# The second norm by token halves, the second modulation's folds moved, and two gate panels in other banks

## The reference

```python
sh1, sc1, g1, sh2, sc2, g2 = jnp.split(jax.nn.silu(c) @ w_mod[l] + b_mod[l], N_MOD, axis=-1)
...
y_att = attend(q, k, v) @ lw['w_attn_o']
y_conv = conformer_conv(u, lw)
merged = jax.nn.sigmoid(ga) * y_att + jax.nn.sigmoid(gc) * y_conv
return merged @ lw['w_out']
...
xs = xs + g1 * token_mixer(hx, lw, rope, k_c, v_c)
hx = modulate(rmsnorm(xs, norm2_g[l]), sh2, sc2)
xs = xs + g2 * peer_ffn(hx, lw)
```

## Time and profile before

| | |
|---|---|
| median of 3 runs | 2541.25 us (2539.21 to 2551.24) |
| the profiled execution: its own time | 2543.47 us |
| its span | 2541.7 us |
| TensorE, VectorE, ScalarE, GpSimd busy | 96%, 66%, 36%, 29% |
| mean granted clock of TensorE | 0.986 |

### The profile page before, as it was taken

One profiled execution on the slowest core, in us unless ns is written; L12 is line 12 of the kernel. 1 busy time (PEld: TensorE's weight loads), 2 busy tenths in 40 slices (PEclk: granted clock), 3 DMA queues, 4 the chain that ended last, 5 costly groups with the idle time before them and its releaser, 6 DMA issues.

```text
span 2541.7 us, 34943 instructions
## 1 busy us (share of the span) xinstructions
PE 2445.8 (96%) x12016; PEld 2073.1 (82%) x12016; DVE 1682.9 (66%) x3129; ACT 911.3 (36%) x1308; POOL 743.7 (29%) x646
## 2 busy tenths in 40 slices
PE   6999999998999999999999999999999989999998
PEld 4877887786887878888777899999999766788886
DVE  4887768788666676777632378888887784444434
ACT  4223852523233333333322333333333564222222
POOL 0000000000025666666675347777741000000000
PEclk8999999999999999999999999999999999999999
DMA  6322913353234444444455589999997212222231
GB/s 256 100 75 98 341 50 127 138 191 141 83 129 137 140 143 140 149 137 145 139 163 166 191 272 363 366 361 359 361 365 279 83 34 67 91 95 95 99 98 59
DMA packets 177222, 433.60 MB, mean 171 GB/s; under 512 B 32752, under 2 KB 81904, under 8 KB 176752
## 3 DMA queue, kind: packets, MB, share of 16 engines
q1 hardware_dynamic: 123888, 331.61, 38.2%
q0 software_dynamic: 34816, 67.41, 7.6%
q10 hardware_dynamic: 18432, 33.56, 3.5%
HBM read 371.48 MB, written 61.01 MB: 170 GB/s over the span
## 4 chain that ended last, share of the span: by engine, by line
PE 82%; DVE 9%; another core or an unknown queue 3%; issue 2%; ACT 2%; DMA 1%; ACTq 0%; SPq 0%; DVEq 0%
PE ps L478 16%; PE ps L480 16%; PE ps L479 16%; PE ps L829 8%; PE ps L831 8%; PE ps L830 8%; DVE wlo L1534 2%; PE ps L736 2%; DVE ar L1587 1%; PE ps L708 1%; ACT whi L1014 1%; PE ps L726 1%; PE ps L548 1%; PE ps L550 1%
## 5 line engine op out<-in xcount | busy, mean ns | idle before, releaser
L1534 DVE TENSOR_TENSOR wlo<-raw,whi 128x1024 fp32r<-128x1024 f32 x426 | 521.4, 1224 | 605.6 <-ACT whi L1014 515.2
L2446 POOL DMA_INDIRECT w_scratch<-ar x384 | 420.9, 1096 | 953.4 <-DVE wlo L1534 849.2
L1014 ACT ACTIVATE whi<-raw 128x1024 fp32r<-128x1024 f32 x424 | 448.8, 1059 | 662.5 <-PE ps L831 348.9
L478 PE MATMUL ps<-b_hi,whi 128*128 128x512 f32 x1312 | 515.8, 393 | 15.8 <-DVE wlo L1534 15.6
L480 PE MATMUL ps<-b_hi,wlo 128*128 128x512 f32 x1312 | 512.6, 391 | 0.8 <-issue 0.8
L479 PE MATMUL ps<-b_lo,whi 128*128 128x512 f32 x1312 | 512.4, 391 | 0.0
L829 PE MATMUL ps<-a_hi,whi 128*128 128x384 f32 x1024 | 344.4, 336 | 6.1 <-issue 3.7
L831 PE MATMUL ps<-a_hi,wlo 128*128 128x384 f32 x1024 | 343.2, 335 | 0.0
L830 PE MATMUL ps<-a_lo,whi 128*128 128x384 f32 x1024 | 343.2, 335 | 0.0
L478 PE MATMUL ps<-a_hi,whi 128*128 128x512 f32 x808 | 323.3, 400 | 6.0 <-DVE wlo L1534 3.3
L480 PE MATMUL ps<-a_hi,wlo 128*128 128x512 f32 x808 | 316.0, 391 | 0.0
(11 more groups left out here) (270 smaller groups left out, 2928.9 us busy)
## 6 DMA issues: line engine op xcount, KB each, us to landing
raw<-panels SPq DMA_DIRECT2D x430, 512.0 KB
w_scratch<-rstd SPq DMA_DIRECT2D x32, 768.0 KB, 10.7
ar<-w_scratch SPq DMA_DIRECT2D x128, 192.0 KB
ar<-gelu_scratch SPq DMA_DIRECT2D x128, 192.0 KB
ar<-mod SPq DMA_DIRECT2D x32, 512.0 KB, 5.3
gelu_scratch<-ar ACTq DMA_DIRECT2D x64, 256.0 KB
gelu_scratch<-sq ACTq DMA_DIRECT2D x32, 256.0 KB
gelu_scratch<-nt ACTq DMA_DIRECT2D x32, 256.0 KB
```

The costliest lines, as they stand in the source:

```text
L478: pe.matmul(bank, w_h, hi[:, k, :], start=(k == 0), stop=False)
L1014: act.activation(whi[:, u % SPLIT, :], raw[:, u % RAW, :], ACT.Copy).then_inc(hi_ready, 1)
L1534: dve.tensor_tensor(wlo[:, u % SPLIT, :], raw[:, u % RAW, :], f32(whi[:, u % SPLIT, :]), ALU.subtract).then_inc(lo_ready, 1)
L2446: nc.gpsimd.indirect_dma_start(experts, bass.IndirectOffsetOnAxis(offs[:, k:k + 1], 0), vals[:, k:k + 1], None)\
```

## The change

Three things change, in one stretch of the program.

1. Gate panels 6 and 7 go to banks 5 and 4, those of the layer norm's sums, and so wait for `cv_stat` and `cv_rt` and for no released gate bank beyond that of panel 5.
2. The folds of the second modulation move forward: pair 4 ahead of the `w_conv_o` loop, pairs 5 to 8 in its turns 0 to 3, pair 9 in turn 5, pairs 10 to 13 in turns 0 to 3 of the `w_out` loop. `mod2_sums(0)` to `(5)` move forward with them, and SP's table `pair_at` too.
3. `w_out` panels 6 and 7 are done by halves of 256 tokens, in the order 6 first half, 7 first half, 6 second half, 7 second half, in four banks (2, 3, 5, 6). The norm's sums, roots, reciprocals, tiles and the first two query panels follow by halves. SP's wait for the keys counts both halves (`4 * KT`); the numbers of later norms go up by one.

The diff, cut to what the prediction speaks of:

```diff
@@ -318,6 +319,10 @@
...
 
+        def gc_bank(k):
+            return k if k < 4 else k - 4 if k < 6 else 11 - k
         def mod2_bank(n):
@@ -409,7 +418,7 @@
...
 
-            pair_at = {3: 2, 4: 3, 8: 4, 9: 5, 11: 6, 12: 7, 13: 8, 14: 9, 19: 10, 20: 11, 21: 12, 22: 13, 23: 14, 24: 15}
+            pair_at = {3: 2, 4: 3, 8: 4, 9: 5, 10: 6, 11: 7, 12: 8, 13: 9, 14: 10, 16: 11, 19: 12, 20: 13, 22: 14, 24: 15}
             for n in range(2 * KT + 4):
@@ -420,7 +429,7 @@
...
 
-            sp.wait_ge(h_ready, 3 * KT)
+            sp.wait_ge(h_ready, 4 * KT)
             sp.dma_start(keys, keys_d).then_inc(keys_in, 16)
@@ -483,27 +492,36 @@
...
 
+            def half_total(half):
+                cols = slice(half * HT, (half + 1) * HT)
+                pe.wait_ge(sq_used, 2 * KT + 6)
+                pe.matmul(ps[:, 4, cols], ones, rstd[:, cols], start=True, stop=False)
+                pe.wait_ge(sq_ready, (3 + half) * KT)
+                pe.matmul(ps[:, 4, cols], ones, sq[:, 0, cols], start=False, stop=False)
+                pe.matmul(ps[:, 4, cols], ones, sq[:, 1, cols], start=False, stop=True).then_inc(sq_used, 8 if half else 2)
             def two_panels(g, hi, lo, free, ready):
 
-                def tile(u, k):
-                    if k == 0:
+                def tile(u, k, half):
+                    cols = slice(half * HT, (half + 1) * HT)
+                    if k == 0 and half == 0:
                         pe.wait_ge(lo_ready, g + u + (1 - U))
...
                     if u == 0:
-                        pe.wait_ge(ready[0], ready[1] + k + 1)
-                    w_h = whi[:, u, k * P:(k + 1) * P]
-                    w_l = wlo[:, u, k * P:(k + 1) * P]
-                    pe.matmul(ps[:, u, :], w_h, hi[:, k, :], start=(k == 0), stop=False)
-                    pe.matmul(ps[:, u, :], w_h, lo[:, k, :], start=False, stop=False)
-                    last = pe.matmul(ps[:, u, :], w_l, hi[:, k, :], start=False, stop=(k == KT - 1))
-                    if k == KT - 1:
+                        pe.wait_ge(ready[0], ready[1] + half * KT + k + 1)
+                    last = split3(ps[:, u, cols], u, k, hi[:, k, cols], lo[:, k, cols], k == 0, k == KT - 1)
+                    if k == KT - 1 and half:
                         last.then_inc(used, 1)
 
-                for s in range(KT + LAG):
-                    if s < KT:
-                        tile(0, s)
-                    if s >= LAG:
-                        tile(1, s - LAG)
+                for half in range(2):
+                    for s in range(KT + LAG):
+                        if s < KT:
+                            tile(0, s, half)
+                        if s >= LAG:
+                            tile(1, s - LAG, half)
+                        if half == 0 and s == 4:
+                            half_total(1)
 
@@ -772,25 +795,39 @@
...
             for k in range(2, KT):
+                if k == 6:
+                    pe.wait_ge(cv_stat, 1)
+                    pe.wait_ge(cv_rt, 1)
                 gate_panel(k)
-            def mod2_sums(q):
-                pe.wait_ge(folds2, (q + 1) * 2 * KT)
-                for n in range(4 * q, 4 * q + 4):
-                    pe.matmul(ps[:, mod2_bank(n), n:n + 1], fold2[:, n % 8, :], ones[:, 0:1], start=True, stop=True).then_inc(summed2, 1)
-            mod2_sums(0)
+                if k == 5:
+                    mod2_sums(0)
+            mod2_sums(1)
             for k in range(KT):
                 panel(CO + k, k % 4, ps[:, k % 4, :], b_hi, b_lo, r_of(CO) + k + 1, (cv_ready, 0) if k == 0 else None)
-                if k in (1, 3, 5):
-                    mod2_sums((k + 1) // 2)
-            for k in range(KT):
+                if k in (2, 4):
+                    mod2_sums(1 + k // 2)
+            def wo_half(k, half):
+                cols = slice(half * HT, (half + 1) * HT)
+                if half == 0:
+                    pe.wait_ge(lo_ready, WO + k + (1 - U))
+                    pe.wait_ge(bank_free, r_of(WO) + k + 1)
+                elif k == KT - 1:
+                    pe.wait_ge(mod_done, 5)
+                for d in range(KT):
+                    last = split3(ps[:, wo_bank(k, half), cols], k, d, a_hi[:, d, cols], a_lo[:, d, cols], d == 0, d == KT - 1)
+                    if d == 3 and k == KT - 2 and half:
+                        half_total(0)
+                last.then_inc(used if half else wo_half_done, 1)
+            for k in range(KT - 2):
                 panel(WO + k, k, ps[:, k % 4, :], a_hi, a_lo, r_of(WO) + k + 1, (m_ready, 0) if k == 0 else None)
-                if k in (3, 5):
-                    mod2_sums((k + 5) // 2)
-            norm_total(2, rstd[:, :])
+                if k in (0, 3):
+                    mod2_sums(4 + k // 3)
+            for half in range(2):
+                for k in (KT - 2, KT - 1):
+                    wo_half(k, half)
             pe.wait_ge(mod_done, 4)
@@ -1286,18 +1323,48 @@
...
 
-            for k in range(KT):
+            for k in range(KT - 1):
                 hi_next(k // 4, WO, k % 4)
...
                     act.activation(tiny[:, 50:51], col("zero"), ACT.Sqrt)
-            act.wait_ge(x_ready, KT)
-            sum_sq_tile(2, KT - 1, rstd[:, :])
-            norm_root(2, rstd[:, :])
+            def half_sq(k, half):
+                cols = slice(half * HT, (half + 1) * HT)
+                act.wait_ge(x_ready, (KT if half else KT - 2) + k - (KT - 2) + 1)
+                act.wait_ge(sq_used, 2 * KT + k - 1)
+                act.activation(sq[:, k % 2, cols], x[:, k, cols], ACT.Square).then_inc(sq_ready, (6 if k == KT - 2 else 2) if half else 1)
+            def half_root(half):
+                cols = slice(half * HT, (half + 1) * HT)
+                act.wait_ge(sq_used, (3 + half) * KT)
+                act.activation(rstd[:, cols], ps[:, 4, cols], ACT.Sqrt, bias=EPS, scale=1.0 / D).then_inc(rt_ready, 1)
+            def half_hi(k, half):
+                cols = slice(half * HT, (half + 1) * HT)
+                act.wait_ge(nt_ready, (2 + half) * KT + k + 1)
+                act.activation(b_hi[:, k, cols], nt[:, k % 2, cols], ACT.Identity, bias=mod[:, 3 * KT + k, 0:1]).then_inc(nhi_ready, 1)
+            half_sq(KT - 2, 0)
+            half_sq(KT - 1, 0)
+            half_root(0)
+            hi_next(1, WO, 3)
+            half_hi(0, 0)
+            half_hi(1, 0)
+            half_sq(KT - 2, 1)
+            half_hi(2, 0)
+            half_hi(3, 0)
+            half_hi(4, 0)
+            half_sq(KT - 1, 1)
             hi(WQ + 1, 1, ((WQ + 1) // 4 + ROUNDS) * 16)
-            norm_hi(2, b_hi, lambda k: mod[:, 3 * KT + k, 0:1])
+            half_hi(5, 0)
+            half_hi(6, 0)
+            half_root(1)
+            half_hi(7, 0)
+            for k in range(KT):
+                half_hi(k, 1)
 
@@ -1888,7 +1955,7 @@
...
             lo(CO + 1, 1)
+            fold_half(2, 0)
 
@@ -1906,7 +1973,9 @@
...
                 if k < 4:
-                    fold_half(2 + k // 2, k % 2)
+                    fold_half((5 + k) // 2, (5 + k) % 2)
+                if k == 5:
+                    fold_half(4, 1)
             merged_lo(KT - 1)
@@ -1932,24 +2001,79 @@
...
 
-            for k in range(KT):
-                if k < KT - 1:
-                    lo(WO + k + 2, k + 2)
+            for k in range(KT - 2):
+                lo(WO + k + 2, k + 2)
                 if k > 1:
...
                 dve.sem_inc(bank_free, 1)
-                if k < 6:
-                    fold_half(4 + k // 2, k % 2)
-                if k == 6:
-                    add_mod2(KT, 2 * KT)
-                    dve.wait_ge(mod_done, 5)
-                    dve.scalar_tensor_tensor(gs2[:, :], mod[:, 4 * KT:5 * KT, 0], 1.0, col("norm2", 0, KT), ALU.add, ALU.mult).then_inc(mod_done, 1)
-                    dve.wait_ge(mod_done, 6)
-            norm_rstd(2)
-            norm_apply(2, x, lambda k: gs2[:, k:k + 1], lambda k: mod[:, 3 * KT + k, 0:1], b_hi, b_lo, middle=lambda: lo(WQ + 1, 1))
+                if k < 4:
+                    fold_half((10 + k) // 2, k % 2)
+            add_mod2(KT, 2 * KT)
+            dve.wait_ge(mod_done, 5)
+            dve.scalar_tensor_tensor(gs2[:, :], mod[:, 4 * KT:5 * KT, 0], 1.0, col("norm2", 0, KT), ALU.add, ALU.mult).then_inc(mod_done, 1)
+            dve.wait_ge(mod_done, 6)
+            add_sq(2, 5, rstd[:, :])
+            def half_add(k, half):
+                cols = slice(half * HT, (half + 1) * HT)
+                if half:
+                    dve.wait_ge(used, WO + k + 1)
+                else:
+                    dve.wait_ge(wo_half_done, k - (KT - 2) + 1)
+                dve.scalar_tensor_tensor(x[:, k, cols], ps[:, wo_bank(k, half), cols], mod[:, 2 * KT + k, 0:1], x[:, k, cols], ALU.mult, ALU.add).then_inc(x_ready, 1)
+                if half:
+                    dve.wait_ge(x_ready, KT + k - (KT - 2) + 1)
+                    dve.sem_inc(bank_free, 1)
+            def half_norm(k, half):
```

(42 more changed lines are left out.)

67 lines of the change are left out of this document (37 added, 30 removed).

## The result

| | before | after |
|---|---|---|
| median of 20 runs each, side by side | 2551.3 us (2539.21 to 2555.88) | 2557.66 us (2542.72 to 2566.78) |
| the profiled execution: its own time, its span | 2543.47, 2541.7 us | 2563.92, 2562.1 us |
| mean granted clock of TensorE | 0.986 | 0.983 |

The ratio is 1.0037, with a 95% interval of 1.0025 to 1.0049: slower, by less than the 0.5% that I had named as telling. Two things are to be kept apart. The median of before, 2541.25 of three runs when the prediction was made, is 2551.3 over twenty, so 10 of the 17 us between forecast and median say nothing of the change. But the sign is wrong as well: forecast -0.6, measured +6.4 as the difference of the two medians, and +9.4 by the ratio.

What follows compares the result with a forecast made beforehand. TensorE, busy for 96% of the span, was taken as the bound, so only pauses and clock could be saved. Delays carried through the stretch summed to -0.6 us; from the median 2541.25 that gave 2540.6 us, range 2535.0 to 2545.5.

Steps and rivals of the forecast that it cites:

- the fold before CO panel 0: Before `w_conv_o` panel 0: TensorE waits 1.8 us for VectorE's second fold, which `mod2_sums(1)` needs.
- between 6a and 7a: In `w_out` by halves: TensorE waits 2.1 us for panel 7's split, with VectorE's low part ending at 582.7.
- the keys' landing: Before the key scores: keys sent at 611.6 land at 616.5, and the scores start at 616.6 against 617.20.
- The step that failed: Over the whole stretch: the sum of -0.6 us takes TensorE's clock as full despite the new pauses.
- the next step: The norm's first half: TensorE starts the query panels at 593.6 against 601.73, and `half_total(1)` ends at 601.5.
- The order of the second total: In the query panels: `half_total(1)` stands two tiles behind tile 0 of panel 1, where TensorE is stopped until 599.0.
- a rival: At the norm: halves run ahead of VectorE and ScalarE, saving waits of 2.1 and 1.5 us; -4.2, 2537.1 us; chance 0.25.
- The clock falls: Around the norm and key scores: TensorE's waits bring 1.2 GHz, +1.0 to +2.9, 2542 to 2544 us; chance 0.15.
- So the gain passes on undiminished: In the selection behind the key scores: waits follow VectorE, 0.7 us earlier at its first fold of pair 7.
- slack that VectorE would eat: At `w_conv_o`: a gain of 0.7 us held as slack is lost when TensorE waits 1.4 us at panel 6.
- The signs: In the changed profile: keys sent near 611.6; wrong if before 609, after 614, or clock at half in 595 to 620.
- The chances: For the whole kernel's time against no change: within 0.5% 0.96, faster by that 0.02, slower by that 0.02.

Runs made afterwards that it cites:

- filled: The changed kernel with four useless matmuls put ahead of the sum before `w_conv_o` panel 0, where TensorE waits for VectorE's fold: ratio 1.0012 to before.
- all three repairs: The changed kernel with the second total earlier, the keys sent at half and four useless matmuls before `w_conv_o` panel 0: ratio 0.9991 to before.
- the two repairs of the chain: The changed kernel with the second total earlier and the keys sent when the norm's first half is done: ratio 1.0003 to before.
- the first part alone: The kernel before with only the moved folds, sums and gate panels' banks, the second norm whole: ratio 0.999 to before, 0.9987 when repeated.
- the second part alone: The kernel before with only the norm, last `w_out` panels and first two query panels by halves; folds, sums, gates as before: ratio 1.003.
- total early: The changed kernel with the second half's total moved just ahead of the first tile of query panel 1: ratio 1.0013 to before.
- keys early: The changed kernel with the keys sent when the norm's first half is done, not both: ratio 1.0013 to before.

## Why the prediction was wrong

**The waits were right.** For the fold before CO panel 0 I had 1.8 us, measured 1.86; for `w_conv_o` panel 6 1.4, measured 1.2; for `w_out` panel 0 0.4, measured 0.2; between 6a and 7a 2.1, measured 1.84; the keys' landing 4.8, measured 4.8. The gate panels' pause is gone. That the pair of `fold_half(2, 0)` lands at about 497 is right too (VectorE waits 1.25 us for it, to 497.35).

**The step that failed** is the one that I had set beside them: "By it, the new pauses may be paid for twice; the sum above takes the full clock." The clock, which the sum took as full, fell in four places behind new pauses: before CO panel 0 (1.6 us), between 6a and 7a (five groups of three matmuls 0.64 apart instead of 0.36, from 585.48 to 588.68, 1.4 us), in the trickling tiles from 599 to 606 (where before had it too, while VectorE set the pace), and behind the keys (0.60 from 622 to 626, 0.4 of 4 us: as much as the 1.6 by which the next stage is longer in after, though with the keys sent early the clock was full and the stage no shorter). The first two, with 0.4 by which this execution is late from the mark on, are the 3.3 us by which TensorE is through `mod2_sums(6)` too late: 596.9 for 593.6. The third is in the next step: "`half_total(1)` stands two tiles behind. It ends at 601.5." It ended at 606.7, 5.2 late: 3.3 that it inherits, and 1.9 of tiles at half pace and of the total itself, 1.9 us for 1.3. From there to the last low part I had 10.0 us, and it took 10.7. So 611.5 became 617.4, and the scores 622.4.

**The order of the second total** is the other half of that term. I saw it stand two tiles behind and took its date, but did not ask what VectorE does until then. Its idle time is in no step as a price; I counted 1.5 us in a rival, and laid them to ScalarE's queue. They were 3.20, and went to 0.70 when the total moved, with ScalarE's queue as it was.

**The rival was named, and priced too low.** "The clock falls" had 0.15 and +1.0 to +2.9 us; the stretch shows +6.3. It left out CO panel 0 and panel 7, the first of which comes at full price: everything that VectorE does in `w_conv_o` and `w_out` hangs on CO panel 0 being done (its loop starts at 504.53, before 502.31, filled 502.54). And I ranked the pauses by length: 1.86 us lay below the 2.61 that kept the clock. It does not go by length alone, nor by the pause alone: behind the same 1.84 us before 7a the clock fell in all five profiles of the whole change without filler, and stayed at 1.00 in both with it. The Trainium skill (TensorE: Matmul & The Clock Gate, A second HAM failure mode: psum-queue depth-cycling) describes a clock that falls through frequent short idle times between groups of matmuls. The trickling tiles of after agree: waits of 0.70, 0.30 and 0.54 us, and matmuls of 0.58 from 599.1 on. Those of all three repairs do not: waits of 0.69, 0.30 and 0.92 us, and a granted clock of 1.00.

**"So the gain passes on undiminished"** failed as well, though no gain came to test it in after: the two repairs of the chain bring the key scores forward by 5.8 us of stretch, and 0.7 go again to the low part behind the fold.

**That the parts gain separately** I had not considered. I held the first part's gain for slack that VectorE would eat; alone it gains 1.5 to 1.7 us of stretch and some 3 us in the runs. In the whole change it is not to be seen, since the clock eats it: with and without it the halves stand at +6.3 and +5.9.

**The signs were right.** I had called it wrong if the keys were sent after 614, "then it is slower than before", or if the clock was at half in 595 to 620; they were sent at 617.50, and the clock was at half in parts of that stretch.

Two slips of the working are small beside this. 1.8 us of waiting from 492.5 and a sum of 0.8 give 495.1 for the start of `w_conv_o`, not 495.4. And before, three sums and not four stand between 495.32 and `w_out` panel 1; the 547.7 us given for it agree with the trace.

The range, 2535.0 to 2545.5, missed for both reasons, either of which was enough: three runs gave a median 10 us under that of twenty, and the mechanism cost 7 us more than the sum. The chances, which went by the difference, gave 0.96 to within 0.5%, and that is where it lies.

What stays open: why the same pauses and trickling tiles keep the full clock once the pause before CO panel 0 is filled, 90 us earlier; why the runs give the second part alone +8.2 us (six runs) where its stretch says +5.9; and why after's first profile was long in the values' part.

## What to carry to other kernels

Splitting a norm so that its consumer can start earlier was no gain here, because the engine that ends last, VectorE, did not end earlier; work started behind a feeder that is no faster became waits, and the clock fell behind some of them. When a reduction feeds another engine's next phase, put it on the queue ahead of whatever waits for that engine: moving one total by nine matmuls was worth 3.1 us, as much as the filler and the clock that it brought back. And a transfer, sent on a counter of the last consumer, may depend in truth only on the last reader of the space that it overwrites.

## What the hardware showed unexpectedly

- A pause of 2.61 us left TensorE's granted clock at 1.00; one of 1.86 us was followed by some 3.5 us at 1.2 GHz, in all seven profiles that have it (after twice, the first part alone twice, total early, keys early, both). The stretch at half begins 0.9 us (keys early) to 2 us (first part alone) behind the pause. Covering the pause with four useless fp32 matmuls kept 1.00, in all four profiles that do.
- The same pause of 1.84 us, 90 us later, was followed by 1.2 GHz in the five profiles without that filler (0.72 to 0.74 from 584 to 590 us) and by the full clock in the two with it (1.00); one of 2.60 us at this place in the second part alone kept 1.00 too. What a pause costs can hang on what stood long before it, and no run here says how.
- Such a matmul of 256 fp32 columns shows two records, which the prediction calls passes, and takes 0.47 us with them (1.89 us for four); twelve of them fill 5 us without moving anything behind them.
- The dense part, 700 us in the same instructions, came out in one of two lengths 1.6 us apart, whatever the kernel. Differences of this size are to be read from the stretch that was changed.
